# Experts of a two-layer diffusion trunk: the loads of the second matrix issued by ScalarE on its own DMA queue

## What is computed

```python
cap = EC_FACTOR * (bsz * n_tok) // N_EXPERTS          # 64 latent tokens, 16 context tokens
aff = softmax(xf @ router, axis=-1)
gate, idx = lax.top_k(aff.T, cap)
xe = xf[idx]
he = silu(einsum('ecd,edf->ecf', xe, w1)) * einsum('ecd,edf->ecf', xe, w3)
ye = einsum('ecf,efd->ecd', he, w2) * gate[..., None]
y = zeros_like(xf).at[idx.reshape(-1)].add(ye.reshape(-1, dm))
```

## Time and profile before

| | |
|---|---|
| median of three runs | 3434.22 us |
| the profiled execution, its own time | 3431.19 us |
| its span, from first to last instruction | 3429.4 us |
| what lies around the span | 1.8 us |
| mean granted clock of TensorE | 0.913 of full speed |
| TensorE matmuls busy | 2655.7 us, 77% |
| VectorE, ScalarE, GpSimd busy | 37%, 14%, 20% |
| experts' phase, layer 0 and layer 1 | from 1092 to 1720 us, from 2782 to 3400 us |

### The profile page before, as it was taken

One profiled execution on the slowest core, in us unless ns is written; L12 is line 12 of the kernel. 1 busy time (PEld: TensorE's weight loads), 2 busy tenths in 40 slices (PEclk: granted clock), 3 DMA queues, 4 the chain that ended last, 5 costly groups with the idle time before them and its releaser, 6 DMA issues. The chain is left out here.

```text
span 3429.4 us, 87591 instructions
## 1 busy us (share of the span) xinstructions
PE 2655.7 (77%) x40000; PEld 2026.6 (59%) x40000; DVE 1272.0 (37%) x2847; ACT 475.1 (14%) x973; POOL 682.5 (20%) x844
## 2 busy tenths in 40 slices
PE   5898884748685888888979988656486858888886
PEld 1555553638535877777725545455485457777774
DVE  1101568784523122211240026686854231112114
ACT  0102332031111000000010023401311100000001
POOL 0000918434220000000010028172440200000001
PEclk9999997869886999999999999977798879999998
DMA  8301000000044988788672010000002458888872
GB/s 353 126 25 37 1 1 11 1 7 28 3 196 156 376 327 327 304 332 330 245 304 70 6 36 1 9 3 7 1 28 88 195 189 337 338 348 328 339 297 100
DMA packets 66320, 532.75 MB, mean 155 GB/s; under 512 B 13952, under 2 KB 15808, under 8 KB 29088
## 3 DMA queue, kind: packets, MB, share of 16 engines
q1 hardware_dynamic: 62880, 516.66, 38.7%
q0 software_dynamic: 3072, 10.49, 1.1%
HBM read 518.34 MB, written 8.79 MB: 154 GB/s over the span
## 5 line engine op out<-in xcount | busy, mean ns | idle before, releaser
L2299 PE MATMUL ps<-arena 128*64 128x80 f32 x16384 | 620.2, 235 | 99.7 <-issue 94.8
L2299 PEld LDWEIGHTS ps<-arena 128*64 128x64 f32 x16384 | 595.4, 139 | 123.0 <-issue 121.3
L2314 PE MATMUL ps<-arena 128*64 128x80 f32 x8192 | 328.8, 236 | 54.9 <-issue 54.9
L2314 PEld LDWEIGHTS ps<-arena 128*64 128x64 f32 x8192 | 309.0, 140 | 65.1 <-issue 65.1
L526 PE MATMUL ps<-arena 128*128 128x128 f32 (+1 forms) x1088 | 296.4, 436 | 5.4 <-DVE arena L579 5.4
L2484 DVE TENSOR_TENSOR arena<-arena,ps 128x160 f32<-128x160 f32 x128 | 41.1, 321 | 645.9 <-ACT arena L2404 645.9
L526 PEld LDWEIGHTS ps<-arena 128*128 128x128 f32 x1088 | 165.0, 192 | 136.8 <-issue 131.1
L2058 POOL DMA_INDIRECT arena<-h_d,arena x32 | 39.8, 1243 | 1024.5 <-DVEq L2425 919.5
L2404 ACT ACTIVATE arena<-ps 128x160 f32<-128x160 f32 x128 | 38.8, 303 | 1128.4 <-PE ps L2299 1128.4
L583 DVE COPY arena<-ps 128x128 f32<-128x128 f32 (+3 forms) x48 | 16.3, 340 | 399.5 <-PE ps L526 287.7
L2444 DVE TENSOR_TENSOR arena<-ps,modc 128x128 f32<-128x128 f32 (+1 forms) x256 | 49.7, 236 | 296.0 <-PE ps L2314 296.0
(11 more groups left out here) (345 smaller groups left out, 4064.9 us busy)
## 6 DMA issues: line engine op xcount, KB each, us to landing
arena<-in_ex_w SPq DMA_DIRECT2D x128, 2048.0 KB, 9.3
arena<-in_ex_w SPq DMA_DIRECT2D x128, 1024.0 KB, 9.0
arena<-in_ada_w SPq DMA_DIRECT2D x24, 2048.0 KB, 15.5
arena<-in_w_t SPq DMA_DIRECT2D x34, 512.0 KB, 3.5
arena<-in_w_tok SPq DMA_DIRECT2D x2, 3712.0 KB, 17.1
h_d<-x_sb SPq DMA_DIRECT2D x10, 512.0 KB, 2.6
arena<-in_w_out SPq DMA_DIRECT2D x2, 2048.0 KB, 7.3
arena<-in_w_uq SPq DMA_DIRECT2D x2, 1536.0 KB, 6.5
```

What stands on the lines that cost most here:

```text
L2299: m = nc.tensor.matmul(gated(j)[c * 64:(c + 1) * 64, f, a, :], w13[q % WG][:, a, k, f * P + c * 64:f * P + (c + 1) * 64], xT[:, x % 2, k, ...
L2314: m = nc.tensor.matmul(product(j)[c * 64:(c + 1) * 64, b, :], w2[:, q % WP, f, b * P + c * 64:b * P + (c + 1) * 64], he[:, x % 2, f, :], s ...
```

## The change

The loads of w2 in the experts' phase, quarters 4 to 63 of each layer, leave SyncE's loop. ScalarE issues each of them on its own queue, after its SiLU of quarter q (and after the copies of `turned` and `turned_context`, where there are any), with the same wait as before on `pr_ps`. The first four quarters of w2 are still loaded by SyncE in the routing phase. The waits for the weights on TensorE, the places and the sizes are as before.

```diff
-def load_w2(e, sp, q, mem):
+def load_w2(e, eng, q, mem):
 
-    sp.dma_start(mem["w2"][:, q % WP].rearrange("p k n -> p (k n)"), e.d["ex_w2"][e.l, q // 4, q % 4].rearrange("p k n -> p (k n)")
+    eng.dma_start(mem["w2"][:, q % WP].rearrange("p k n -> p (k n)"), e.d["ex_w2"][e.l, q // 4, q % 4].rearrange("p k n -> p (k n)")
                  ).then_inc(e.S[f"ld_f{q % WP}"], 16)
...
                 if q + WG < QUARTERS:
                     sp.wait_ge(S["h_ps"], q + 1)
                     load_w13(e, sp, q + WG, mem)
-                if q >= WP:
-                    sp.wait_ge(S["pr_ps"], q - WP + 1)
-                    load_w2(e, sp, q, mem)
             sp.wait_ge(S["xe_used"], NE)
...
                         if i == HALF - 1:
                             turned_context(0)
+                    if x:
+                        act.wait_ge(S["pr_ps"], q - WP + 1)
+                        load_w2(e, act, q, mem)
             turned(NI - 1)
```

## The result

The changed kernel takes 3439.47 us, median of 17 runs (3422.18 to 3443.98), against 3430.5 us for the kernel before on the same chips (17 runs, 3420.28 to 3435.6). The ratio is 1.0022, 95% interval 1.0012 to 1.0032: slower by 7.5 us by the ratio and by 9.0 between the medians, where 121 us were forecast.

A forecast was written before the change was run, and what follows sets the result against it. It took late instruction fetches, held up by load data in the experts' phase, to bound the kernel. 3431.2 us profiled + 117 for the second data queue + 4 for early chunks gave 3552 us; range 3440 to 3610.

The forecast's parts named there:

- What bounds the kernel: Experts' phase: TensorE's stops before gate and w2 products are instruction fetches made late by load data, not waits for weights.
- price of 129 us: Both full windows of the experts' phase: 22528 matmuls would take 975 us instead of 1104 without late fetches.
- quiet window: Stretch after the gate loads end, DMA share 0.40: 1063 matmuls in 46 us, 43.3 ns each, used as yardstick.
- Point 1: 60 load issues a layer move from SyncE to ScalarE, covered by its waits: 0, at most 1 us in the whole.
- point 2: The wait on `pr_ps` on ScalarE's queue ends a whole gate before the next SiLU can begin: cost 0.
- Point 3: Two data queues in the experts' phase: w2 goes ahead of fetches that fall into gate loads; 117 us, from 0 to 175.
- point 4: Chunks of `ada_w` go out earlier and fill the window 1648 to 1694: net +4 us, between 0 and +10.
- term of 2.46 us a fetch: Extra wait for one w2 load by each fetch in a gate load; 0.78 fetches a quarter, 1.9 us at first.
- arithmetic of the quarter: Quarter length with stops shrinking as it lengthens: 10.9 us, 1.49 more, 175 us over 118 quarters.
- first rival: q8 keeps its turn, so fetches in gate loads wait as today: about +20, 3451 us, 3440 to 3480; chance 0.22.
- second: No difference: a fetch waits for all data posted, whatever its queue; only the early chunks cost, 3435 us; chance 0.13.
- fourth rival: Faster: two loads alternate packet by packet, so fetches wait 0.9 us; half of 129 us goes, 3366 us; chance 0.08.

The follow-up runs named there:

- alltiny: Kernel before with every gate and w2 load in the experts' phase cut to 256 bytes a partition, all issues, waits and matmuls kept; 3238.79 us, ratio 0.9434.
- swap: Against the kernel before: ScalarE issues the gate loads and SyncE those of w2, chunks of ada_w still behind w2; 3434.91 us against 3429.56, ratio 1.0014.
- both: Against the kernel before: half of every gate and w2 load issued on SyncE's queue, half on ScalarE's, at the same event; ratio 1.0023.
- split21: Kernel before with every gate load in two DMAs of 1 MB, w2 loads whole, all posted at once on SyncE's queue; ratio 1.0024.
- one_early: Kernel before, all loads on SyncE's queue, but five chunks of ada_w issued early, each when its gate is done; ratio 1.0018.
- ticks42: Kernel before with loads in 512 KB pieces on SyncE's queue, one issued per TensorE signal after each group of 32 matmuls; ratio 1.0105.
- paced422: Kernel before with loads in 512 KB pieces, SyncE waiting for the last but one to land before issuing each; 3978.16 us, ratio 1.1598.

## Why the prediction was wrong, point by point

*What bounds the kernel.* Right. `alltiny` shows that the stops go with the load data (one of 116 is left), and 194 us go with the data in all, of which 147 are listed stops. That they are instruction fetches is shown by the 1.2 to 1.6 us between the end of a fetch and that of a stop, in each of the 116. The price of 129 us was too low, since the quiet window holds more of the long matmuls.

*Point 1, the issues on ScalarE, and point 2, the wait on its queue.* Right: 0.33 us each, and no SiLU waits for anything but its gate product.

*Point 3, the second data queue.* **This step failed.** It forecast 117 us from 175, on the ground that a fetch gets its turn at the end of a load's share and that w2 on another queue could go first. In the changed kernel the idle time before gates and products of w2 grew by 8.3 us in all, of which part is point 4's. The ground itself was wrong: a turn is one row, so a fetch waits at most 0.61 us for its turn, and w2 on another queue adds no 2.46 us to it. `swap` sets the order against the fetch, `both` doubles what the queues compete with, `split21` halves the share that a turn could hold, and none of them moves the stops (156.9, 152.5 and 152.4 us against 149.7) by more than a few us. The reading rested on one fetch, and on windows in which packets of all 16 DMA engines are mixed: on its own engine even that fetch had two rows of the gate load behind it. The term of 2.46 us a fetch is nothing, so the arithmetic of the quarter has nothing to work on.

*Point 4, the early chunks.* Right in mechanism: the stretch filled up and got stops, the products behind it got part of that back, and the next phase didn't gain. The size fits as far as it can be told: +4 us, 0 to 10, was forecast, and `one_early` has 6 us (1 to 11).

*The rivals.* The time came out as the first rival, q8 keeps its turn, at its lower edge, and as the second, no difference but point 4 (3435 us against 3439.47). `swap` excludes the first in the form that goes by the queues' order, and turns of one row exclude it in both forms. The second is the one that held, in the sense of the Trainium skill (DMA: Bandwidth & Descriptors, Issuing engines are not separate DMA queues): loads from several issuers interleave on the same DMA engines, and what is saved is the time to issue. These runs agree, with 1.0010 (0.9997 to 1.0024) for the second queue alone and rows that alternate one by one. Its argument in the prediction, that a fetch waits for all data posted, isn't shown by any run: `ticks42` doesn't speak against it and `paced422` only leans its way. What counted for it was that bytes, rates and issue times stay the same. The objection that I put against it was the one wrong reading again. The fourth rival, with 0.08 for turns packet by packet, had the size of a turn right and the consequence wrong: the stops stayed, because they aren't waits for a turn.

*The chances.* The cases "no difference" and "q8 keeps its turn" had 0.35 together. The rule on turns of the Trainium skill's page was taken as borne out by one row of the trace, with a load's share for a turn; in that reading the packets' times contradict it. With two theories for a single row, the forecast should have been the one whose sum needs no new mechanism.

**What stays open.** Why a fetch comes so late while data flow. The time passes before its packet starts: the packet itself takes no longer than without data, and a stop ends 1.2 to 1.6 us after it in every version, with at most three exceptions in each but `paced422`. It isn't a turn among the queues, nor their number or order, nor the size of a DMA from 256 KB to 2 MB, nor the rows from 2 to 16 KB. That leaves the flow of data as such (112 us of stops with w2's data gone, next to none with all gone) and the amount in flight (some 8 us of them in `paced422`, where both were lower). `ticks42` lowered the amount alone, from 3.1 to 2.2 MB, without effect; further apart the two were never moved.

## What to carry to other kernels

A second queue for the loads of the same stage is worth nothing when the issues were covered and the loads are early; look for what else the move releases on the queue that is left, as here the chunks, which went out up to 48 us sooner into the one quiet stretch. A program of many small instructions pays for its instruction fetches while loads keep the DMA engines 0.86 busy (some 150 us of idle time here), and neither splitting, nor pacing at full rate, nor spreading the loads over queues lowered it by more than 12 us; fewer bytes did, and so did two pieces in flight, at a rate that cost 548 us. To tell whether a stop is a fetch, compare its end with the end of the last packet of q8. And before a mechanism is put on one pair of rows, look for a row elsewhere in the trace that it forbids; a window that mixes 16 DMA engines doesn't show what stands next to what on one of them.

## What was not expected of the hardware

- Two busy queues take turns row by row on a DMA engine, in the order q1, q8, q10 (34 fetches of 91 between a gate row and a row of w2 after the change, one the other way round), and a fetch stands in the middle of a load as a rule (64 of 96 before).
- A stop ends 1.2 to 1.6 us after the end of the fetch's packet, which itself takes 1.05 us with load data and 1.06 without.
- The fetches' lateness is hardly affected by how the load data are cut or queued: stops of 138 to 169 us in eleven kernels (the two of the change among them), one queue or two, against 111.6 with a third of the data gone and 2.4 with nearly all gone.
- Two pieces of 512 KB in flight moved only 219 GB/s, where loads of 1 and 2 MB posted freely move 330 and peak at 426.
- Rows of 2 KB keep the DMA engines busy for 0.94 of the time at 322 GB/s, rows of 8 and 16 KB for 0.86 at 330.
